# Front tokens of the feed-forward stages: one 512-column matmul per high weight tile, two sums in one bank

## The reference

```python
def swiglu(x, w_in, w_out):
    gate, up = jnp.split(x @ w_in, 2, axis=-1)
    return (jax.nn.silu(gate) * up) @ w_out

for i in range(2):
    x = x + 0.5 * swiglu(rmsnorm(x, ffn1_norm[i]), ffn1_w_in[i], ffn1_w_out[i])
    x = x + mixer_i(rmsnorm(x, mix_norm[i]))            # layer 0: S5, layer 1: HGRN2
    x = x + cross_attend(rmsnorm(x, xattn_norm[i]), mem_k[i], mem_v[i], ...)
    x = x + 0.5 * swiglu(rmsnorm(x, ffn2_norm[i]), ffn2_w_in[i], ffn2_w_out[i])
y = rmsnorm(x, final_norm)
```

## Time and profile before

| what | value |
|---|---|
| time, median of 3 runs | 2359.36 us |
| profiled execution, span of the core | 2357.9 us (1.5 us less than the median; the profile does not say which time it had itself) |
| mean granted TensorE clock | 0.998 of full speed |
| TensorE matmul busy | 2332.7 us, 21043 matmuls |
| TensorE weight load busy | 2270.3 us |
| VectorE busy | 1295.9 us, 1906 instructions |
| ScalarE busy | 869.0 us |
| GpSimd busy | 609.4 us |

### The profile page before, as it was taken

How to read it: one execution, slowest core, us unless ns; L and a number is a source line. 1 busy time by engine, 2 the same in 40 slices (tenths; PEclk the granted TensorE clock), 3 DMA queues, 4 the chain that set the end, 5 groups by cost and what they waited for, 6 DMA issues and landing times.

```text
span 2357.9 us, 50146 instructions
## 1 busy us (share of the span) xinstructions
PE 2332.7 (99%) x21043; PEld 2270.3 (96%) x21043; DVE 1295.9 (55%) x1906; ACT 869.0 (37%) x1399; POOL 609.4 (26%) x591
## 2 busy tenths in 40 slices
PE   8999999999999999999999999999999999999999
PEld 8999999889979999999999999999999979999999
DVE  6653643964576443445543344577777666443443
ACT  4422333453233321322433233267775233321323
POOL 4779967331103000004111010432122102000003
PEclk9999999999999999999999999999999999999999
DMA  6455445553562333333543333233332653333332
GB/s 167 128 161 149 123 134 169 171 170 107 166 242 84 98 99 91 96 96 99 158 117 111 100 108 115 83 100 108 104 111 77 213 188 91 97 94 94 98 94 94
DMA packets 483707, 289.19 MB, mean 123 GB/s; under 512 B 22289, under 2 KB 466962, under 8 KB 482514
## 3 DMA queue, kind: packets, MB, share of 16 engines
q1 hardware_dynamic: 477856, 280.66, 40.4%
q0 software_dynamic: 560, 1.84, 0.6%
q10 hardware_dynamic: 5122, 4.25, 0.5%
HBM read 258.86 MB, written 27.85 MB: 122 GB/s over the span
## 4 chain that ended last, share of the span: by engine, by line
PE 90%; DVE 4%; POOL 2%; ACT 1%; issue 1%; DMA 1%; SPq 0%; DVEq 0%; POOLq 0%; ACTq 0%
PE lin L3021 51%; PE lin L3026 25%; PE mis L2512 4%; POOL sTmp L737 1%; PE mis L2650 1%; PE lin L2600 1%; PE lin L2762 1%; PE mis L2633 1%; PE lin L2757 1%; PE lin L2983 1%; POOL sGe L738 0%; DVE w_lo L1827 0%; POOL sFe L738 0%; PE lin L2650 0%; PE mis L2626 0%
## 5 line engine op out<-in xcount | busy, mean ns | idle before, releaser
L1827 DVE TENSOR_TENSOR w_lo<-raw,w_hi 128x1024 fp32r<-128x1024 f32 (+1 forms) x322 | 464.0, 1441 | 294.4 <-ACT w_hi L1330 293.7
L1330 ACT ACTIVATE w_hi<-raw 128x1024 fp32r<-128x1024 f32 (+1 forms) x328 | 365.1, 1113 | 314.2 <-PE lin L3026 244.4
L3021 PE MATMUL lin<-a_rear,w_hi 128*128 128x264 f32 x3552 | 455.6, 279 | 0.0
L3021 PE MATMUL lin<-a_front,w_hi 128*128 128x256 f32 x3552 | 451.5, 279 | 1.1 <-DVE a_rear L1840 0.7
L3021 PEld LDWEIGHTS lin<-a_rear,w_hi 128*128 128x128 f32 x3552 | 432.6, 188 | 0.0
L3021 PEld LDWEIGHTS lin<-a_front,w_hi 128*128 128x128 f32 x3552 | 424.4, 188 | 4.5 <-issue 1.8
L3026 PE MATMUL lin<-a_rear,w_lo 128*128 128x264 f32 x1776 | 245.1, 278 | 0.0
L3026 PE MATMUL lin<-a_front,w_lo 128*128 128x256 f32 x1776 | 240.5, 277 | 1.0 <-DVE w_lo L1827 1.0
L2391 DVE SCALAR_TENSOR_TENSOR xT<-lin,xT 128x520 f32<-128x520 f32 (+1 forms) x87 | 60.9, 700 | 322.8 <-PE lin L3026 322.1
L1063 POOL TENSOR_TENSOR acc<-xT 128x520 f32<-128x520 f32 x8 | 12.2, 1521 | 864.6 <-DVE xT L2391 836.6
L3026 PEld LDWEIGHTS lin<-a_rear,w_lo 128*128 128x128 f32 x1776 | 223.8, 188 | 0.0
(11 more groups left out here) (512 smaller groups left out, 3181.5 us busy)
## 6 DMA issues: line engine op xcount, KB each, us to landing
raw<-in_ffn_w_in_dram SPq DMA_DIRECT2D x176, 512.0 KB, 3.9
raw<-in_ffn_w_out_dram SPq DMA_DIRECT2D x64, 704.0 KB, 4.6
kc<-in_cache_mem_k_dram SPq DMA_DIRECT2D x32, 512.0 KB, 7.1
vc<-in_cache_mem_v_dram SPq DMA_DIRECT2D x16, 1024.0 KB, 9.1
raw<-in_hg_w_in_dram SPq DMA_DIRECT2D x32, 512.0 KB, 4.3
raw<-in_xattn_w_kv_dram SPq DMA_DIRECT2D x16, 512.0 KB, 4.4
raw<-in_s_w_glu_dram SPq DMA_DIRECT2D x16, 512.0 KB, 4.0
raw<-in_xattn_w_q_dram SPq DMA_DIRECT2D x16, 512.0 KB, 3.9
```

The source lines that it names most:

```text
L1330: act.activation(w_hi[:, j, 0:kt, :], raw[:, j, 0:kt, :], ACT.Copy).then_inc(hi_ready, 1)
L1827: dve.tensor_tensor(low_weights(n, j), raw[:, j, 0:kt, :], w_hi[:, j, 0:kt, :].bitcast(F32), ALU.subtract).then_inc(lo_ready, 1)
L3021: pe.matmul(lpart(j, half), high[:, k, :], (x_lo if u else x_hi)[half][:, k, :], start=start and u == 0 and k == 0, stop=False)
```

## The change

The two front tensors become one, `both`, with the high tokens in `[:, 0]` and the low ones in `[:, 1]`; they lie where they lay. In every FFN stream except the first pair of the first one, a high weight tile meets high and low front tokens in one matmul of 512 columns, which fills the whole first bank of `lin[:, j]`: high x high in columns 0 to 255, high x low in 256 to 511. The low weights still add to columns 256 to 511. The rear half, the other dense products, and all loads of weights from memory stay. VectorE adds the two front sums: in an input projection columns 0 to 255 are multiplied by `rstd` into a part of `sqt`, and that is added to `t1` or `t4`; in an output projection a second scalar_tensor_tensor adds columns 0 to 255 to `xT`, ahead of the one that was there.

```diff
@@ -178,19 +178,20 @@
     def split_tokens(name, kt, offset):
 
         step = kt * FRONT
-        front = [at(f"{name}_front_{e}", [P, kt, TF], F32R, offset + e * step) for e in range(2)]
+        both = at(f"{name}_front", [P, 2, kt, TF], F32R, offset)
+        front = [both[:, e] for e in range(2)]
         offset += 2 * step
         rear = [at(f"{name}_rear_{e}", [P, kt, REAR // 4], F32R, offset + e * kt * REAR)[:, :, 0:TR] for e in range(2)]
-        return tuple((front[e], rear[e]) for e in range(2))
+        return tuple((front[e], rear[e]) for e in range(2)) + (both,)
 
     xT = at("xT", [P, KD, NT], F32, o_x)
-    a_hi, a_lo = split_tokens("a", KD, o_ah)
+    a_hi, a_lo, a_both = split_tokens("a", KD, o_ah)
     raw = at("raw", [P, 2, FH, P], F32, o_raw)
     w_hi = at("w_hi", [P, 2, FH, P], F32R, o_wh)
     w_lo8 = at("w_lo8", [P, 2, KD, P], F32R, o_wl)
     FREE_LOW = 2 * KD - FH
     w_lo11 = [at(f"w_lo11_{j}", [P, FH, P], F32R, o_wl + j * (2 * KD - FH) * P * 4) for j in range(2)]
-    f_hi, f_lo = split_tokens("f", FH, o_hid)
+    f_hi, f_lo, f_both = split_tokens("f", FH, o_hid)
     HTILE = FRONT + REAR
     h_hi = at("h_hi", [P, KD, HTILE // 4], F32R, o_hid)[:, :, 0:NT]
     h_lo = at("h_lo", [P, KD, HTILE // 4], F32R, o_hid + FH * HTILE)[:, :, 0:NT]
@@ -385,6 +386,10 @@
 
     def lflat(j):
         return lin[:, j].rearrange("p a n -> p (a n)")[:, 512 - TF:512 + TR]
+
+    def lfront_sums(j):
+
+        return lin[:, j, 0, :].rearrange("p (e n) -> p e n", e=2)
@@ -2346,7 +2351,7 @@
                 def body(p, i, first, last):
                     inner = not (first or last or unrolled(n))
                     if inner:
-                        step.loop(i, 1, 1 if is_in(name) or name == "glu" else 0)
+                        step.loop(i, 1, 3 if is_in(name) else 2 if name[:3] == "ffn" else 1 if name == "glu" else 0)
                     for j in range(2):
                         if (j == 0 or not first or r is None) and not (name == "hg_out" and first and j == 0):
                             if not late_low(n, j, last):
@@ -2361,13 +2366,23 @@
                             return
                         dve.wait_ge(chunk_done, 2 * p + j + 1)
                         m = 2 * i + j
+                        parted = name[:3] == "ffn" and not (first and r == 0)
                         if is_in(name) and j == 0:
                             wait(dve, gate_out, g0 + i)
-                            dve.tensor_tensor(t1[:], lflat(0), rstd[:], ALU.mult).then_inc(used[0], 1)
+                            if parted:
+                                dve.tensor_tensor(sqt[:, 0:TF], lin[:, 0, 0, 0:TF], rstd[:, 0:TF], ALU.mult)
+                                step.link(dve.tensor_tensor(t1[:], lflat(0), rstd[:], ALU.mult))
+                                dve.tensor_tensor(t1[:, 0:TF], t1[:, 0:TF], sqt[:, 0:TF], ALU.add).then_inc(used[0], 1)
+                            else:
+                                dve.tensor_tensor(t1[:], lflat(0), rstd[:], ALU.mult).then_inc(used[0], 1)
                             if not first:
                                 hidden_lo(i - 1)
                         elif is_in(name):
+                            if parted:
+                                dve.tensor_tensor(sqt[:, TF:2 * TF], lin[:, 1, 0, 0:TF], rstd[:, 0:TF], ALU.mult)
                             step.link(dve.tensor_tensor(t4[:], lflat(1), rstd[:], ALU.mult))
+                            if parted:
+                                step.link(dve.tensor_tensor(t4[:, 0:TF], t4[:, 0:TF], sqt[:, TF:2 * TF], ALU.add))
                             dve.wait_ge(gate_out, g0 + i + 1)
                             dve.tensor_tensor(t3[:], t4[:], t2[:], ALU.mult).then_inc(used[1], 1)
                             if last:
@@ -2388,6 +2403,9 @@
                         else:
 
                             scale = 0.5 if name[:3] == "ffn" else 1.0
+                            if parted:
+                                step.link(dve.scalar_tensor_tensor(out=tile(xT, m)[:, 0:TF], in0=lin[:, j, 0, 0:TF], scalar=scale,
+                                                                   in1=tile(xT, m)[:, 0:TF], op0=ALU.mult, op1=ALU.add))
                             dve.scalar_tensor_tensor(out=tile(xT, m), in0=lflat(j), scalar=scale,
                                                      in1=tile(xT, m), op0=ALU.mult, op1=ALU.add)\
                                 .then_inc(used[j], 1)
@@ -2423,6 +2441,9 @@
             def last_tile(half):
                 cols = COLS[half]
                 dve.wait_ge(chunk_done, 2 * ALL_PAIRS + half)
+                if half == 0:
+                    step.link(dve.scalar_tensor_tensor(out=xT[:, KD - 1, cols], in0=lin[:, 1, 0, 0:TF], scalar=0.5,
+                                                       in1=xT[:, KD - 1, cols], op0=ALU.mult, op1=ALU.add))
                 dve.scalar_tensor_tensor(out=xT[:, KD - 1, cols], in0=lpart(1, half), scalar=0.5, in1=xT[:, KD - 1, cols],
                                          op0=ALU.mult, op1=ALU.add).then_inc(used[1], 1)
                 dve.wait_ge(squares_done, NORMS)
@@ -3017,6 +3038,12 @@
                     high, low = w_hi[:, j], low_weights(n, j)
 
                     def high_weights(half, u, ks, start):
+                        if name[:3] == "ffn" and half == 0:
+                            if u == 0:
+                                for k in ks:
+                                    pe.matmul(lfront_sums(j), high[:, k, :], (f_both if hidden else a_both)[:, :, k, :],
+                                              start=k == 0, stop=False)
+                            return
                         for k in ks:
                             pe.matmul(lpart(j, half), high[:, k, :], (x_lo if u else x_hi)[half][:, k, :],
                                       start=start and u == 0 and k == 0, stop=False)
@@ -3079,9 +3106,13 @@
                     wait(pe, used[1], p)
                     low = low_weights(n, 1)
                     for half in range(2):
-                        for u, x in enumerate((x_hi, x_lo)):
+                        if half == 0:
                             for k in range(kt):
-                                pe.matmul(lpart(1, half), w_hi[:, 1, k, :], x[half][:, k, :], start=u == 0 and k == 0, stop=False)
+                                pe.matmul(lfront_sums(1), w_hi[:, 1, k, :], f_both[:, :, k, :], start=k == 0, stop=False)
+                        else:
+                            for u, x in enumerate((x_hi, x_lo)):
+                                for k in range(kt):
+                                    pe.matmul(lpart(1, 1), w_hi[:, 1, k, :], x[1][:, k, :], start=u == 0 and k == 0, stop=False)
                         if half == 0:
                             pe.wait_ge(lo_ready, 2 * p + 2)
                         else:
```

## The result

The change made the kernel **slower**: 2388.14 us median of 4 runs (2385.00 to 2389.88), beside 2359.78 for the kernel before on the same chip, a ratio of 1.0116 (95% interval 1.0103 to 1.0129). The forecast was 2350.1 us, with a range of 2340 to 2359.5; the measured time lies 29 us above the range.

A forecast was written before the change was run, and what follows sets the result against it. The prediction took TensorE's matmul queue as the bound; -14.0 us from merging and +0.5 + 1.4 + 1.0 + 1.4 + 0.4 us of waits and lost saving gave -9.3, from 2359.4 to 2350.1 us, range 2340 to 2359.5.

The forecast's parts named there:

- By it a 512-column matmul takes 213.3 + 6.7 = 220 ns: FFN front matmuls: each of 2096 merges takes 220 ns in place of 226.7, saving 14.0 us in all.
- The bound from below: Merged matmuls' least gain: a moving operand of two memory stretches pays the fixed part twice, and nothing goes.
- The attention rows: Attention scores, another type, 216.2 ns each, as upper bound on the merge's gain: 10.5 ns each, 21.9 us in all.
- rival D: Merged matmuls: two stretches cost as much as two matmuls, only VectorE's joins are left, +4.7 us, 2364; chance 0.10.
- The waits (4.7 us with what is lost at GpSimd): TensorE's unhidden waits behind VectorE's joins, plus saving lost before GpSimd's tables: 0.5 + 1.4 + 1.0 + 1.4 + 0.4 us.
- the 1.0 us for the first layer: First layer, split ending at 113.23: the join delays it by 0.8 to 1.3, so TensorE waits 1.0 us.
- Rival E: Twice the waits with the forecast spacing, joins slowed wherever GpSimd works: 9.4 us of waits, 2354.8; chance 0.06.
- A chain that runs at its own speed: GpSimd's tables, awaited before 195.46, keep their own pace, so 0.4 us saved by six chunks before is lost.
- PSUM is given back far earlier than TensorE returns to it: Input projection loops: TensorE returns to PSUM only a chunk of 5.5 us later, part of the 0.8 us being hidden.
- the block ends: Last output tile before the second layer, S5 mixer and HGRN2: extra VectorE instruction unhidden, 3 x 0.45 = 1.4 us.
- the 1.4 us forecast: Second layer's FFN a, just after the norm: VectorE still catching up after the reciprocal, TensorE waits 1.4 us.
- Rival F: Loops: the join outlasts the 1.76 us there; 87 pairs wait 0.24 each, 21 us, 2371; chance 0.04.

The follow-up runs named there:

- contig: Changed kernel with high and low front tokens of each contraction tile side by side, so a merged matmul's 512 columns are one stretch of memory; 2390.93 us.
- stretches: The `joins` kernel with each 256-column matmul taking 128 high and 128 low front tokens, two stretches at the old width; 2373.04 us.
- joins: Changed kernel with its two sums and VectorE's additions kept, but 256-column matmuls as before in place of merged ones; 2376.02 us, ratio 1.0075.
- nojoin: Changed kernel with merged matmuls but without VectorE's additions of the two sums, the first sum left unused; 2371.61 us, ratio 1.0056.
- halfrows: Changed kernel with the 512-column matmuls contracting over only the first 64 of 128 rows; 2484.65 us.
- halfcols: Changed kernel with all 512-column matmuls except the first of a sum using only 64 of the weight tile's 128 columns; 2392.92 us.

## Why the prediction was wrong, point by point

- **"By it a 512-column matmul takes 213.3 + 6.7 = 220 ns"** is the step that failed. Its ground was that the fixed part does not depend on width, read from two widths eight columns apart. The measured fixed part is 19.4 to 20 ns at 512 columns. The mechanism, TensorE's spacing as the bound, was right; the term's size and sign were not: -14.0 is +12.4 us, an error of 26.4. The bound from below was wrong as well: "nothing goes" was taken as the worst, though no row excluded a loss. The attention rows were no bound either; they have another type.
- The point from which the change loses, 224.4 ns, was right to name; rival D's condition was met (232.6), but not its mechanism: two stretches cost nothing (contig, stretches). The rule of the Trainium skill (TensorE: Matmul & The Clock Gate, "Back-to-back issue gap") gives 215.8 ns at 512 columns; the trace does not agree here either, by 17 ns.
- **Second-order loss, not forecast:** some 4 us of low-weight and rear matmuls in the output loops, whose spacing grew by 4 to 8 ns behind merged ones.
- **The waits (4.7 us with what is lost at GpSimd) were mis-sized:** alone the joins cost 13.8 by the spans. The term that failed is the 1.0 us for the first layer. Its one place came as forecast (1.12 us before 118.24), but I had read one place of that FFN and not its others: 1.75 before 151.44, 1.19 before 303.92, and seven from 0.25 to 0.90. The product and the split slow down beside GpSimd, and the wait for ScalarE's high weights was in no row I had looked at, since before it ended in time everywhere. Rival E (twice the waits) had the right mechanism, and was still too small.
- **"A chain that runs at its own speed"** The earlier trace rows was wrong: GpSimd's tables start behind VectorE's `mg_lo`, 4.1 us later in joins and 5.0 in the change. That the loss ahead of them is swallowed came true, but the second wait for tables grew by 1.9 us (joins).
- **"PSUM is given back far earlier than TensorE returns to it"** holds in the loops and not behind the reciprocal: three waits for the first bank, 0.53 us each in joins, 1.6 us that no term had.
- What held: the loops hide the join (0.00 in joins); the price of an instruction, 0.42 to 0.43 us; from input to output projection nearly nothing; at the block ends before the second layer and before HGRN2 TensorE waits 0.66 us, and +0.46 and +0.45 are seen in joins, as forecast. The rest of the second layer's first FFN came near the 1.4 us forecast in its sum alone, by luck: of +1.8 us in joins the low weights make 0.68, the bank 0.53 and high weights 0.33. VectorE in the loop, in place of the earlier trace rows:

```profile
972.25 0.42 DVE L2382 TENSOR_TENSOR sqt<-lin,rstd 128x256 f32<-128x256 f32 x1 [1.11 <-PE lin L3053]
972.59 0.69 DVE L2383 TENSOR_TENSOR t<-lin,rstd 128x520 f32<-128x520 f32 x1
973.31 0.43 DVE L2385 TENSOR_TENSOR t<-t,sqt 128x256 f32<-128x256 f32 x1
973.86 0.70 DVE L2387 TENSOR_TENSOR t<-t,t 128x520 f32<-128x520 f32 x1
```

The product starts 1.61 us after the sum is there, against 0.82 before, the 0.8 forecast; TensorE does not wait for what follows. Rival F falls with it.

The parts fit the whole within their intervals: by the ratios 17.7 and 13.2 us make 30.9 of 27.4; by the spans of the profiled executions 13.8 and 7.9 make 21.7 of 25.3. Brought to the two stretches at half clock that the kernel before has (the change has one, joins two, nojoin none), the spans give 13.8 and 11.1, 24.9 of 26.9. Open is why the fixed part grows with width, why it alternates, and whether it does so for another type than float32r, which no run tried.

## What to carry to other kernels

A cost per instruction that two nearly equal widths show alike is not thereby constant: before merging matmuls for it, time one of the new width. For this type, widths up to 264 columns paid 6.7 ns each and 512 paid about 20, so fewer and wider was worse than two of 256. Work put on an engine that is off the critical path has to be checked at every place where that engine feeds the path, above all where it already runs slower beside another, and where a third engine starts behind it; a quarter of the joins made over two thirds of what they cost. Before stages of two profiles are subtracted, the granted clock has to be compared stretch by stretch: a mean of 0.998 and one of 0.999 hid 1.6 us.

## What the runs showed of the hardware that was not expected

- The steps of the fixed part: 6.7 ns at 256 and 264 columns, 12.7 at 288, about 13 up to 384, 16.0 at 448, 19.4 at 512.
- A matmul of 64, 128 or 192 columns among wide ones adds 111 to 113 ns to what the wide one costs in a row of its own, as much as one of 256 columns (113.3).
- TensorE's granted clock was 0.50 for short stretches behind waits as short as 0.89 and 0.45 us, and each cost some 1.6 us (before, 196.5 and 415.0; joins, 219.5).
- A wait of TensorE for weights cost 0.27 us more than the idle time that the profile shows (joins, 251.80 and four more).
- A change between contraction heights costs some 200 ns each time. In halfrows a row of 64-row matmuls goes between 128-row ones:

```profile
967.63 2.82 PE L3044 MATMUL lin<-f_front,w_hi 64*128 64x512 f32 x11
970.39 1.53 PE L3053 MATMUL lin<-f_front,w_lo 128*128 128x256 f32 x11
971.76 1.45 PE L3053 MATMUL lin<-f_rear,w_lo 128*128 128x264 f32 x11
```

Eleven take 2.76 us in place of 2.56 and the eleven behind them 1.37 in place of 1.25 to 1.30. In the single records four spacings are some 90 to 110 ns too long: the last ahead of the row (208 instead of 117), the first (333) and the last (317 to 323) of the row, and the first behind it (223); the others are not. Over the 238 rows (174 in input, 64 in output projections) that makes some 93 us, nearly all of the 96. Half the columns of the weight tile (halfcols) cost nothing of the kind.
